# Three experts' rows added by one-hot products, a seventh expert slot, written-out expert loops: one change to a decoder layer on one core

## The reference

```python
combine = jnp.sum(jax.nn.one_hot(e_idx, N_EXPERTS) * w_sel[..., None], axis=1)
y = jnp.zeros_like(u)
for e in range(N_EXPERTS):                       # 32 experts, D_EXPERT = 256
    hid = jax.nn.silu(u @ w1[e]) * (u @ w3[e])   # 1024 -> 256, twice
    y = y + combine[:, e:e + 1] * (hid @ w2[e])  # 256 -> 1024
return h + y
```

## Time and profile before

| | us |
|---|---|
| runs | 656.86, 651.99, 657.08 |
| the profiled execution: its own time | 656.88 |
| its span, first to last instruction | 655.3 |
| tables ready, first gather issued (L847) | 378.12 |
| first `expand` starts | 385.77 |
| last `expand` starts | 623.11 |
| last DVE instruction ends | 652.22 |

### The profile page before, as it was taken

How to read it: one execution, slowest core, us unless ns; L and a number is a source line. 1 busy time by engine, 2 the same in 40 slices (tenths; PEclk the granted TensorE clock), 3 DMA queues, 4 the chain that set the end, 5 groups by cost and what they waited for, 6 DMA issues and landing times.

```text
span 655.3 us, 9228 instructions
## 1 busy us (share of the span) xinstructions
PE 586.7 (90%) x3489; PEld 400.9 (61%) x3489; DVE 238.1 (36%) x552; ACT 226.7 (35%) x431; POOL 138.1 (21%) x225
## 2 busy tenths in 40 slices
PE   8799999998999997999999879999999877779840
PEld 7688788895665563666887635655555554445520
DVE  3644335233654873583926711111111110111106
ACT  6725415253554443673526402121112111111110
POOL 8100002110232221144200112223232212221110
PEclk9799799998999997999999869999999999999985
DMA  8910000006000012000976639999999999999929
GB/s 249 389 60 1 0 2 1 0 12 264 1 1 1 0 47 92 1 2 0 383 290 258 261 130 372 375 394 388 390 395 379 398 396 389 392 394 399 362 87 351
DMA packets 35811, 136.02 MB, mean 208 GB/s; under 512 B 8808, under 2 KB 10904, under 8 KB 26816
## 3 DMA queue, kind: packets, MB, share of 16 engines
q1 hardware_dynamic: 29536, 124.92, 49.8%
q0 software_dynamic: 5664, 8.55, 4.2%
q10 hardware_dynamic: 576, 2.10, 0.8%
HBM read 131.28 MB, written 12.65 MB: 220 GB/s over the span
## 4 chain that ended last, share of the span: by engine, by line
PE 68%; SPq 10%; DMA 9%; DVE 7%; issue 4%; ACT 2%; POOL 0%; ACTq 0%; POOLq 0%; DVEq 0%
PE ps L1810 15%; PE ps L2140 12%; PE ps L2167 5%; PE ps L1996 5%; PE ps L1886 5%; PE ps L1941 5%; PE ps L1985 5%; DMA w<-in_w 4%; SPq L636 3%; PE ps L2099 3%; SPq L637 3%; SPq L643 3%; DMA w_in_ffcq<-in_w_in 2%; DMA yg<-y_rows 2%; PE ps L1746 2%
## 5 line engine op out<-in xcount | busy, mean ns | idle before, releaser
L2140 PE MATMUL ps<-w,xt 128*64 128x256 f32 x1024 | 121.2, 391 | 24.2 <-issue 20.0
L2140 PEld LDWEIGHTS ps<-w,xt 128*64 128x64 f32 x1024 | 79.7, 141 | 75.2 <-issue 46.5
L1673 DVE TENSOR_TENSOR xt<-ps,g_ffn_c 128x512 f32<-128x512 f32 x32 | 22.1, 691 | 211.5 <-PE ps L2099 211.5
L1203 ACT ACTIVATE hsb<-ps,row_scale 128x256 f32<-128x256 f32 x32 | 15.1, 473 | 136.6 <-PE ps L2140 136.6
L2167 PE MATMUL ps<-w,hT 128*64 128x512 f32 x256 | 61.8, 604 | 0.0
L847 POOL DMA_INDIRECT xg<-h_rows,idx x32 | 30.3, 946 | 126.5 <-PE ps L2099 114.6
L837 POOL DMA_INDIRECT y_rows<-yh,idy x32 | 32.6, 1019 | 77.9 <-ACT yh L1222 77.9
L777 POOL TENSOR_SCALAR_AFFINE_SELECT probT<-probT 128x128 f32<-128x128 f32 (+2 forms) x80 | 23.3, 309 | 92.4 <-ACT probT L1122 91.8
L1996 PE MATMUL ps<-probT,vals 128*128 128x512 f32 (+4 forms) x160 | 42.6, 410 | 0.0
L1985 PE MATMUL ps<-qT,kT 68*128 68x400 f32 (+9 forms) x160 | 42.1, 407 | 0.0
L2099 PEld LDWEIGHTS ps<-ident,xg 64*128 64x128 f32 x256 | 30.6, 199 | 15.4 <-issue 15.4
(11 more groups left out here) (309 smaller groups left out, 941.7 us busy)
## 6 DMA issues: line engine op xcount, KB each, us to landing
w<-in_w SPq DMA_DIRECT2D x96, 1024.0 KB, 25.9
yg<-y_rows SPq DMA_DIRECT2D x4, 1024.0 KB, 7.9
x<-in_x SPq DMA_DIRECT2D x4, 512.0 KB, 5.5
w_in_v<-in_w_in SPq DMA_DIRECT2D x1, 2048.0 KB, 11.1
w_in_k<-in_w_in SPq DMA_DIRECT2D x1, 2048.0 KB, 15.9
w_in_q<-in_w_in SPq DMA_DIRECT2D x1, 2048.0 KB, 20.7
w_oa<-in_w_o SPq DMA_DIRECT2D x1, 2048.0 KB, 8.9
w_ob<-in_w_o SPq DMA_DIRECT2D x1, 2048.0 KB, 8.3
```

Of the source, the lines that this page charges most:

```text
L2140: ins = pe.matmul(ps[j * slots:(j + 1) * slots, 2 + b, 0:F], xt[b][:, k, :], w13[s][:, j, k, :], start=(k == 0), stop=(k == DK - 1))
```

## The change: what it does

1. **A seventh slot.** `RING` is 7. The new slot's w1 and w3 lie where `mixT` was, its w2 in the region of the router's tables. w1 of expert 6 is asked for right behind w2 of expert 4, w3 of expert 6 behind expert 5, and w2 of expert 6 once the tables have been read (`tables_read`), which is now a wait in SP's order ahead of every later load. Small buffers (`xg`, `xt`, `yh`, `hsb`, `idx`, ...) move elsewhere; `yg[0..2]` now lie in slot 5's place, `yg[3]` in the new slot.
2. **Loops written out.** PE, DVE and SP have all 32 experts as straight code.
3. **The last three experts are not scattered.** `KEPT = 3`, `SENT = 29`. For experts 29, 30 and 31 ACT copies the result scaled by a weight for each slot (`slot_coef`) into `y_hi` (float32r), and DVE writes the remainder `y_lo`. DVE builds one-hot tables `kept_hot` in the steps of experts 27 to 29, PE turns them in those of 28 to 30 (`turn_kept`, four transposes each), ACT copies them to `comb`. At the end PE forms `comb` times `y_hi` and `y_lo` for all four token tiles (`combine`, 48 products of 512 columns) into all eight banks, and DVE adds them to `x` (`add_kept`). SP waits only for the scatters of the first 29 experts before it loads `yg`.
4. **Rows that nobody scatters must be zero.** In the middle of the kernel, behind the first attention's masks, POOL clears a tile and writes 4 MB of zeros to `y_rows`; `y_zeroed` is awaited by ACT ahead of `split_high(0)` and by POOL ahead of the gathers.
5. **`keep_warm(7, 18)` instead of 8** ahead of the first expert, and `slot_coefs` (eight small products) behind the first expert's `turn_hidden`; DVE has five small operations more ahead of the first expert, and copies `slot_coef` behind `hT` of expert 0, which is what sets `tables_read`.

```diff
-RING = 6
+RING = 7
+KEPT = 3
+SENT = NE - KEPT
...
+            step(pool.memset(zeros[:, :], 0.0))
+            pool.dma_start(y_rows.rearrange("(p r) d -> p r d", p=P),
+                           zeros[:, :].unsqueeze(1).to_broadcast([P, 2 * SEQ // P, D])).then_inc(y_zeroed, 16)
...
             sp.dma_start(w2s[4][:, :, :], w2_v[4]).then_inc(w2_in[4], 16)
+            sp.dma_start(w13[6][:, 0, :, :], w1_v[6]).then_inc(w13_in[6], 16)
             sp.wait_ge(wo_done, 2 * NT)
             sp.dma_start(w13[4][:, 0, :, :], w1_v[4]).then_inc(w13_in[4], 16)
             sp.dma_start(w13[4][:, 1, :, :], w3_v[4]).then_inc(w13_in[4], 16)
             load_expert(5, 5)
+            sp.dma_start(w13[6][:, 1, :, :], w3_v[6]).then_inc(w13_in[6], 16)
+            sp.wait_ge(tables_read, 1)
+            sp.dma_start(w2s[6][:, :, :], w2_v[6]).then_inc(w2_in[6], 16)
+            for e in range(RING, NE):
+                load_w13(e)
+                if e > RING:
+                    load_w2(e - 1)
+            load_w2(NE - 1)
...
             for b in range(2):
-                sp.wait_ge(y_stored[b], 16 * NE // 2)
+                sp.wait_ge(y_stored[b], 16 * ((SENT + 1 - b) // 2))
...
+            def store_rows(e):
+                b = e % 2
                 act.wait_ge(y_done, e + 1)
+                if e >= SENT:
+                    k = e - SENT
+                    act.activation(y_hi[k][:, :], ps[:, 6 + b, :], ACT.Copy, scale=slot_coef[:, k:k + 1]
+                                   ).then_inc(y_copied, 1)
+                    return
...
+            def split_rows(k):
+                e = SENT + k
+                dve.wait_ge(y_copied, e + 1)
+                dve.scalar_tensor_tensor(out=y_lo[k][:, :], in0=ps[:, 6 + e % 2, :], scalar=slot_coef[:, k:k + 1],
+                                         in1=y_hi[k][:, :].bitcast(F32), op0=ALU.mult, op1=ALU.subtract
+                                         ).then_inc(y_split, 1)
+            dve_turned(0)
+            for e in range(NE):
+                if e < NE - 1:
+                    dve_turned(e + 1)
+                dve_gate(e)
+                if e == 0:
+                    dve.wait_ge(coefs_turned, 1)
+                    dve.tensor_copy(slot_coef[:, :], ps[:, COUNT, NE:NE + KEPT]).then_inc(tables_read, 1)
+                if SENT - 2 <= e < NE - 2:
+                    keep_hot(e - SENT + 2)
+                if e > SENT:
+                    split_rows(e - SENT - 1)
+            split_rows(KEPT - 1)
...
+            def add_rows(t):
+                dve.wait_ge(tile_in[t], 32)
                 for k in range(2):
+                    step(dve.scalar_tensor_tensor(out=x[:, t, :], in0=yg[t][:, k, :], scalar=coef[:, t, k:k + 1],
+                                                  in1=x[:, t, :], op0=ALU.mult, op1=ALU.add))
+            def add_kept(t):
+                dve.wait_ge(combined, t + 1)
+                dve.tensor_tensor(x[:, t, :], x[:, t, :], pair(2 * t, D), ALU.add).then_inc(out_made, 1)
+            for t in range(NT - 1):
+                add_rows(t)
+            add_kept(0)
+            add_kept(1)
+            add_rows(NT - 1)
+            add_kept(2)
+            add_kept(3)
...
             pe.wait_ge(over_made, 1)
-            keep_warm(7, 8)
+            keep_warm(7, 18)
+            turn_gathered(0)
+            for e in range(NE):
+                expand(e)
+                if e < NE - 1:
+                    turn_gathered(e + 1)
+                turn_hidden(e)
+                if e >= 1:
+                    contract(e - 1)
+                if e == 0:
+                    slot_coefs()
+                if SENT - 1 <= e < NE - 1:
+                    turn_kept(e - SENT + 1)
+            contract(NE - 1)
...
+            def combine(t, k):
+                for q in range(2):
+                    rows_q = slice(q * slots, (q + 1) * slots)
+                    for n, part in enumerate((y_hi[k], y_lo[k])):
+                        ins = pe.matmul(ps[:, 2 * t + q, :], comb[k][rows_q, t * P:(t + 1) * P], part[rows_q, :],
+                                        start=(k == 0 and n == 0), stop=(k == KEPT - 1 and n == 1))
+                return ins
+            pe.wait_ge(comb_made, KEPT)
+            pe.wait_ge(y_split, KEPT - 1)
+            for k in range(KEPT - 1):
+                for t in range(NT - 1):
+                    combine(t, k)
+            pe.wait_ge(y_split, KEPT)
+            for t in range(NT - 1):
+                combine(t, KEPT - 1).then_inc(combined, 1)
+            for k in range(KEPT):
+                ins = combine(NT - 1, k)
+            ins.then_inc(combined, 1)
```

More of the change, by code:

```diff
@@ L242, in build @@
         kT = place("kT", [MLA_AUG, H, L], F32, r_qk + H * SEQ * 4)
-        yg = [place(f"yg{t}", [P, 2, D], F32, r_qk + 8192 * t) for t in range(NT)]
         PAIRS = H // 2
@@ L250, in build @@
         r_moe = r_u + 512
+        yg = [place(f"yg{t}", [P, 2, D], F32, ring + 8192 * t if t < NT - 1 else r_moe) for t in range(NT)]
         assert r_qk + 2 * SLOT <= r_moe
@@ L253, in build @@
         mix_lo = [place(f"mix_lo{b}", [P, DK // 2, SEQ], F32R, r_moe + DK // 2 * SEQ * 4 * b) for b in range(2)]
-        xg = [place(f"xg{b}", [slots, DK, P], F32, r_moe + 4096 * b) for b in range(2)]
-        xt = [place(f"xt{b}", [P, DK, slots], F32, r_moe + 8192 + 2048 * b) for b in range(2)]
-        yh = [place(f"yh{b}", [P, D // 2], F32, r_moe + 12288 + 2048 * b) for b in range(2)]
+        w13.append(place(f"w13_{RING - 1}", [P, 2, DK, F], F32, r_moe))
         r_l = region((QRK * SEQ + KVRK * L) * 4)
@@ L287, in build @@
         scrap = place("scrap", [P, D], F32, r_s)
+        yh = [place(f"yh{b}", [P, D // 2], F32, r_s + 2048 * b) for b in range(2)]
+        ysb = place("ysb", [slots, D], F32, r_s)
+        hsb = [place(f"hsb{b}", [P, F], F32, r_s + 4096 + 1024 * b) for b in range(2)]
+        w2s.append(place(f"w2_{RING - 1}", [P, FK, D], F32, r_p))
+        assert r_p + FK * D * 4 <= r_s
         st_fox = [place(f"st_fox{b}", [P, H, FOX_AUG], F32, r_s + ST * b) for b in range(2)]
@@ L404, in build @@
         eps_made, dve_gf = sem("eps_made"), sem("dve_gf")
-        x_in = [sem(f"x_in{t}") for t in range(NT + 1)]
+        tile_in = [sem(f"tile_in{t}") for t in range(NT + 1)]
         win_in = {b: sem(f"win_in_{b}") for b in BLOCK_ORDER}
@@ L855, in _ @@
                     scatter_rows(e - LAG)
-            for e in range(NE - LAG, NE):
+            for e in range(NE - LAG, SENT):
                 scatter_rows(e)
@@ L1199, in copy_hidden @@
                     act.wait_ge(scales_made, 1)
-                if not first or s >= 2:
+                if e >= 2:
                     act.wait_ge(h_turned, e - 1)
@@ L1245, in _ @@
+            store_rows(NE - 1)
             act.wait_ge(over_made, 1)
@@ L2142, in expand, with turn_hidden @@
                 ins.then_inc(h13_done, 1)
-            def turn_hidden(it, s, first=False):
-                e = it * RING + s
-                b = s % 2
+            def turn_hidden(e):
+                b = e % 2
                 pe.wait_ge(hs_out, e + 1)
-                if not first or s >= 2:
+                if e >= 2:
                     pe.wait_ge(hT_made, e - 1)
+                if e == 1:
+                    pe.wait_ge(tables_read, 1)
                 for m in range(FK):
```

304 lines of the change are left out of this document (139 added, 165 removed).

## The result

| | before | after |
|---|---|---|
| median of 20 runs each | 656.86 us | 653.41 us |
| lowest and highest | 651.99 to 658.05 | 648.72 to 656.28 |
| ratio after/before, 95% | | 0.9941 [0.9925, 0.9957] |
| the profiled execution | 656.88, span 655.3 | 652.52, span 650.9 |

The change gains 0.6%: less than the 1% that the prediction took for no change, but the interval lies clear of 1. The median is 0.01 us above the range given. What follows is about the 5.4 us that are missing from the forecast.

The account below looks back on a forecast made before the run. The prediction held the expert stage bound by the weights' DMA stream, with an unhidden tail behind it. Terms -5.4 - 0.3 + 0.4 - 3.6 = -8.9 us gave 648.0 us; range 643.0 to 653.4.

Parts of the forecast that it names:

- Start of the stream: Head, up to SP's first load of the stream: starts 0.4 us later than 392.25, at 392.6.
- a gather that slips by 0.5: First gather, beside 1 MB more of weights: +0.5 us, taken from a range of 0 to +2.7.
- `expand(0)` at full clock: First expert's `expand` on PE: eighteen `keep_warm` products keep the clock up, -2.8 us; 0 if the clock falls.
- rule on packets: DMA engines take queues in turn, packet by packet, so the gather's +2.7 us end would not occur; no term of the sum.
- both slips of the head: Before the stream: the clock falls before `expand(0)` and the gather lands with the last weights; 653.0 us, within a 0.15 rival.
- The wait for `tables_read`: SP's queue after `expand(0)`: waits until 392.6, holding all further loads; counted in the stream's +0.4 us start.
- Bytes in the stream: Expert weight stream: 25.33 experts loaded in place of 26, -5.4 us; expert 29's scatter gone, -0.3 us.
- Tail: From T, the start of the last `expand`, to the span's end: T+28.6 in place of T+32.2, -3.6 us.
- Costed at nothing: Zeros, small DVE and POOL work, transposes and one-hots, written-out loops: hidden in idle time or saving nothing, 0 us.
- late instructions: Written-out experts: eight more instruction packets fetched beside the weights' stream stall PE; 668 us, chance 0.07.
- stall at the jump: Tail: the jump over the slow path stalls, costing 2.4 or 3 us; 650 to 651 us, chance 0.10.
- the first rival: Head of the stream slips: clock falls (650.8 us), gather lands with the last weights (+2.2 more), or both (653.0); chance 0.15.

Follow-up runs that it names:

- b2: Changed kernel with w2 of expert 5 and w3 of expert 6 held until the first gather lands, expert 7's w1 and w3 ahead of the `tables_read` wait; 643.23 us.
- c2: b2 with the last `yg` tile scaled by ACT and added by POOL, while DVE adds the other three; 644.4 us, 0.9815 of before.
- c3: b2 with w1 and w3 of expert 5 held back too, so all of expert 5 waits for the first gather; 649.44 us, 0.9883 of before.
- c4: b2 with w1 and w3 of expert 6 loaded only once `expand(0)` is done, so six experts are ahead; 646.4 us, 0.9851 of before.
- a2: Changed kernel with w1 and w3 of expert 7 asked for ahead of the wait for `tables_read`; 648.6 us, 0.9889 of before.
- b3: Changed kernel with w1 and w3 of expert 6 loaded only once `expand(0)` is done, so six experts are ahead; 653.3 us, 0.9946 of before.
- a3: Changed kernel with all 32 experts scattered and the old tail, no one-hot products; 656.15 us, 0.9995 of before.
- a4: Kernel before the change with its three expert loops written out, nothing else changed; 656.44 us, 0.9999 of before.

## Why the prediction was wrong, point by point

- **Start of the stream: the step that failed.** The forecast was +0.4 us, as the sum of a gather that slips by 0.5, `expand(0)` at full clock (-2.8), and 2.7 from there to the load. Measured, from the gather's issue on: gather +2.8, `expand(0)` -1.0, wait 3.3, together +5.0; in the span, which the earlier issue does not shorten, the gather lands 1.4 later for 0.5, and the first load goes out 3.7 later for 0.4. The step argued that the gather is served beside the weights, and took 0.5 of a range of 0 to 2.7. It lands behind the last weights, and against the kernels with 5 MB the sixth costs 1.6 to 2.0. What probably misled was the kernel before: there the first packet of the gather came 2.2 us after its issue, when the weights were nearly through, and the short time in which both queues moved can be read as service beside them. Nor does the rule on packets exclude the other end, as the prediction has it: by the estimate above one packet can last as long as the gather waited. That end was in the text as a rival, with 653.0 us for both slips of the head, but at a chance of 0.15, when all of it slipped at once.
- **`expand(0)` at full clock** is the term that missed by most in the span, 1.8 us (the landing 0.9, the wait 0.6). The working put the last of the eighteen products at 383.4, just ahead of the turning, from the half clock of the eight in the earlier trace rows. Here they started at full clock, took 4.06 and ended at 379.8, the gather landed at 385.1 and not at 384.2, and the clock was down by 384. All runs divide in the same way: where PE was idle for at most 0.53 us ahead of the turning (b2, c2, c3, c4) `expand(0)` took 3.67, where it was idle for 2.46 us or more 5.31 to 6.47. How long the eighteen products take was not the same in each execution: 4.06 us in seven of the ten kernels that have them, 5.6 to 6.9 in b2, c3 and c4.
- **The wait for `tables_read`** was seen, and seen to hold up all loads behind it; its length was forecast as 2.7 from the end of `expand(0)`, measured 3.3, as `slot_coefs` ends behind ACT's part and not beside it. That a wait which costs only 0.4 in the sum is a real 3 us, to be had by asking for expert 7 ahead of it, the prediction did not draw; a2 did.
- **Bytes in the stream:** -5.7 with the scatter, measured -4.8. b3 against after gives 230.4 - 226.1 = 4.3 for the slot, and over all traces it is 4.1 to 5.3, where its bytes were put at 5.4. a3, which scatters expert 29 as well, needs 225.9 us from the first load to T, so the 0.3 of that scatter do not show. So the term was about 1 us too large. Why stays open: the rate in the stream is the same, and no run was made for it.
- **Tail:** T+28.6 forecast, T+28.9 measured. The split took 0.75 (0.7), the hole behind it, with the load of `over`, its test and the jump, 0.73 (0.5, from 0 to 2.4), six adds 7.89 (7.64), two from banks 2.35 (2.56). The store behind DVE is 3.2 (3.1). Scatter, landing and `yg` are off the path, as said; a3 confirms it with 3.5 us.
- **Costed at nothing:** the zeros take 12.3 us of transfer under POOL's work in a stretch that moves nothing else. No run leaves them out alone. What they could delay is the issue of the first gather: it lies at 374.2 to 379.6 in the twelve traces with them and at 376.45 and 378.12 in the two without (a4, before), and a3, which has them, stands at 0.9995, so that little is left for them. Written-out loops: right, by a4.
- **Rivals:** late instructions, the way to 668 us, did not happen; eight transfers more, as estimated, cost nothing (a4). The tail did not stall at the jump. What happened is the first rival, together with a stream that gained 0.9 less.
- **The first gather's issue** lay 1.37 us earlier in the profiled execution than before's: the output projection ended 0.6 earlier, and ten products in the router, at half clock in before, ran at full clock. Neither comes from the change: a4 shows both too (376.45). The profiled pair gives -4.4, the medians -3.4.

**The best version** is b2_hold_2mb, 0.9788 [0.9770, 0.9807] of before: the change with two MB of weights held until the first gather has landed, and the loads of expert 7 ahead of the wait. The profiled execution of b2 shows a G to T of 238.19 and c2, with the same head, 235.04: b2's eighteen products ran at half clock for most of their 6.86 us (below) and ended 2.7 behind the gather. b2's median is 643.23.

## What to carry to other kernels

A small transfer that something waits for should not be issued behind megabytes that nobody needs yet: hold back as much as is still moving when it is issued (2.4 MB in the changed kernel, of which b2 held 2), and no more than fits behind it ahead of the next loads, since beyond that the engines stand still and the stream starts late (b2 against c3). And when a change lets a queue run further ahead, price the queue's new length at the next small transfer behind it, and look which waits of the issuing engine stand ahead of loads that could go.

## What was not expected of the hardware

- A gather of 64 rows on the software queue takes 3.5 to 3.9 us when at most 0.4 MB of weights are left on the hardware queue at its issue, 5.6 to 6.9 with 1.0 to 1.5 MB, and 8.4 to 8.6 with 2.4 to 2.5. Its first packet comes 1.7 us after the issue where nothing else moves (c3), and 4.3 after it beside 412 GB/s of weights.
- Eighteen products that started at half clock in one execution and at full clock in another took 6.86 us in b2 and 4.06 in c2, which has the same head. In c3 the granted clock fell with PE at work, from 1.00 in the window 368 to 369 to 0.52 in the next, both with PE busy all the time, and the products of the router that follow took nearly twice as long (2.80 for 1.53 us). No edit here is seen to decide which of the two an execution gets.

```profile
368.00:369.00 1.00, 1.00 (x12) 1.00 (x11) 0.93 (x6) 0.97 (x3) 0.00 (x0) 1.00 1.12 418
369.00:370.00 1.00, 1.00 (x7) 1.00 (x7) 0.69 (x6) 0.98 (x2) 0.08 (x1) 0.52 1.00 315
```

- DVE and POOL adding at the same time out of the same memory slow each other: one add of DVE 3.24 in place of 1.30 us (c2). The Trainium skill (SBUF — State Buffer, section SBUF: two separate sides) says that of a DVE operation with two inputs in SBUF and a POOL operation one holds the shared ports and the other waits; the rows agree: POOL's two adds take 3.16 each, the first from 628.47 to 631.6; DVE's add starts 1.0 us into it and ends 1.1 behind it, near the 1.30 that it takes alone.
- The load of `over`, its test and the taken jump together cost DVE 0.73 us, between the end of its last split and its first add. The jump alone is not shown.
